# A token-projection stage whose weight units are loaded and split in halves, with its gates' row in three parts

## The reference

```python
def hybrid_layer(x, ...):
    h = rmsnorm(x, norm_pre_mix)
    proj = _f32(h @ w_in)
    u, z, xbc, dt_raw, qk, v, i_raw, f_raw, o_raw = jnp.split(proj, [int(o) for o in offs], axis=-1)
    y_a = s5_mixer(u, ...)                 # diagonal state space, then g * sigmoid(g @ w_glu + b_glu)
    y_b = ssd_mixer(z, xbc, dt_raw, ...)   # dt = softplus(dt_raw + dt_bias); acs = cumsum(dt * a, axis=2)
    y_c = mlstm_mixer(qk, v, i_raw, f_raw, o_raw, ...)   # log_sigmoid(f_raw + b_f), cumsum, running max
    mix = jnp.concatenate([y_a, y_b, y_c], axis=-1).astype(x.dtype) @ w_out
    x = x + rmsnorm(mix, norm_post_mix)
    h = rmsnorm(x, norm_pre_ffn)
    ff = (jax.nn.silu(h @ w_gate) * (h @ w_up)) @ w_down
    return x + rmsnorm(ff, norm_post_ffn)
```

## Time and profile before

| | us |
|---|---|
| median of 3 runs | 3132.67 |
| lowest, highest | 3131.85, 3136.79 |
| the profiled execution: its time | 3131.07 |
| the profiled execution: its span | 3129.3 |
| token stage, first to last matmul of its products | 577.3 to 1151.0 |
| PE busy, whole span | 2893.2 (92%) |
| DVE, ACT, POOL busy | 1905.5, 1198.4, 389.7 |
| mean granted TensorE clock | 0.964 of full speed |

### The profile page before, as it was taken

One profiled execution on the slowest core, in us unless ns is written; L12 is line 12 of the kernel. 1 busy time (PEld: TensorE's weight loads), 2 busy tenths in 40 slices (PEclk: granted clock), 3 DMA queues, 4 the chain that ended last, 5 costly groups with the idle time before them and its releaser, 6 DMA issues. The chain is left out here.

```text
span 3129.3 us, 35939 instructions
## 1 busy us (share of the span) xinstructions
PE 2893.2 (92%) x13608; PEld 2329.2 (74%) x13608; DVE 1905.5 (61%) x2572; ACT 1198.4 (38%) x1965; POOL 389.7 (12%) x495
## 2 busy tenths in 40 slices
PE   7999999689999775999789949999999999999998
PEld 4888887567776554777668848888878888888887
DVE  4777877565652216788434357666676666565756
ACT  5322222444342424455333344333443333454543
POOL 0000000013440006566202110000000000000100
PEclk9999999889999887999989979999999999999999
DMA  4222432336654537877477764444453222676863
GB/s 146 65 68 86 135 127 101 109 122 201 210 192 145 146 102 255 268 264 271 168 273 279 286 217 170 155 161 163 167 183 128 101 101 105 236 268 194 295 191 113
DMA packets 290105, 545.14 MB, mean 174 GB/s; under 512 B 58732, under 2 KB 150284, under 8 KB 276492
## 3 DMA queue, kind: packets, MB, share of 16 engines
q1 hardware_dynamic: 258172, 437.69, 41.4%
q0 software_dynamic: 24704, 75.52, 6.7%
q10 hardware_dynamic: 7056, 29.63, 2.4%
HBM read 358.30 MB, written 184.44 MB: 173 GB/s over the span
## 5 line engine op out<-in xcount | busy, mean ns | idle before, releaser
L2390 PE MATMUL f_banks<-f_bop,f_w_op 128*128 128x512 f32 x3696 | 842.9, 390 | 31.8 <-DVE f_w_op L2217 29.6
L2390 PEld LDWEIGHTS f_banks<-f_bop,f_w_op 128*128 128x128 f32 x3696 | 696.5, 189 | 178.2 <-DVE f_w_op L2217 30.0
L2398 PE MATMUL f_banks<-f_d_op 128*128 128x512 f32 x1848 | 419.0, 389 | 0.0
L2398 PEld LDWEIGHTS f_banks<-f_d_op 128*128 128x128 f32 x1848 | 346.8, 188 | 72.0
L1130 PE MATMUL t_banks<-t_w_hi,h_hi 128*128 128x512 f32 (+1 forms) x640 | 249.5, 390 | 31.7 <-DVE t_w_lo L1005 31.7
L2281 DVE TENSOR_TENSOR f_d_op<-f_d_raw,f_d_op 128x1024 fp32r<-128x1024 f32 x154 | 187.3, 1225 | 149.1 <-ACT f_d_op L2134 148.6
L640 PE MATMUL c_banks<-h_hi,c_w_hi 128*128 128x512 f32 x640 | 255.8, 400 | 0.0
L640 PE MATMUL c_banks<-h_hi,c_w_lo 128*128 128x512 f32 x640 | 249.9, 390 | 0.0
L640 PE MATMUL c_banks<-h_lo,c_w_hi 128*128 128x512 f32 x640 | 249.1, 389 | 0.0
L1130 PE MATMUL t_banks<-t_w_hi,h_lo 128*128 128x512 f32 (+1 forms) x640 | 239.6, 374 | 0.0
L1130 PE MATMUL t_banks<-t_w_lo,h_hi 128*128 128x512 f32 (+1 forms) x640 | 239.3, 374 | 0.0
(11 more groups left out here) (350 smaller groups left out, 4599.1 us busy)
## 6 DMA issues: line engine op xcount, KB each, us to landing
f_raw<-in_w_gu SPq DMA_DIRECT2D x88, 512.0 KB, 6.4
sop<-f_a SPq DMA_DIRECT2D x154, 256.0 KB, 2.0
f_d_raw<-sop SPq DMA_DIRECT2D x154, 256.0 KB, 2.8
t_raw<-in_w_tok SPq DMA_DIRECT2D x36, 1024.0 KB, 5.5
f_d_raw<-top SPq DMA_DIRECT2D x88, 256.0 KB, 4.2
m_bc<-rows SPq DMA_DIRECT2D x16, 1152.0 KB, 6.8
f_d_raw<-in_w_dn SPq DMA_DIRECT2D x66, 256.0 KB, 3.1
o_y_hi<-y_hi SPq DMA_DIRECT2D x16, 1024.0 KB, 5.1
```

Of the source, the lines that this page charges most:

```text
L2390: last = nc.tensor.matmul(bank[:, g, :], w_op[:, t % W_RING, w, cols], bop[:, s, h, k, :], start=begins and k == 0 and j == 0, stop=k == 3 ...
L2398: last = nc.tensor.matmul(banks[:, bank, :], d_op[:, d % D_RING, s, tok], d_op[:, d % D_RING, w, :], start=k == 0 and j == 0, stop=k == FU ...
```

## The change

Three things are changed in `phase_tokens`.

1. *Halves.* Load, `upper` and `lower` of a unit work on two halves of 1024 columns, first half in slot t=0, second half in slot t=1 of the unit ahead. There is a semaphore for the landing of each half (`raw_in[half]`), and `whi_ok` and `wlo_ok` count halves. A half of `t_raw` is loaded again as soon as `lower` has read that half. PE waits for the first half before the unit's first matmul, and in its first slot again before the first matmul that uses the second half.
2. *The row in three parts.* DVE's operations of slot 9c+0 are dealt out to slots 9c+0 (L1023 to L1037), 9c+1 (L1038 to L1046) and 9c+3 (L1048 to L1057), with the halves of `lower` in between where the slots fall on t=0 or t=1.
3. *Exponentials.* ACT's Ln and four Exp stand in slot 9c+5 instead of 9c+6, and both places with Exp and Ln load one table set that has both functions. That load stands behind the wait for `abs_ok` or `args_ok`.

The diff, without the changes of declaration:

```diff
@@ -805,10 +806,11 @@
 
         @block.sync
         def _(sp):
-            def load(unit):
+            def load(unit, half):
+                cols = slice(half * 2 * NB, (half + 1) * 2 * NB)
                 if unit:
-                    sp.wait_ge(wlo_ok, unit)
-                sp.dma_start(raw[:], w_tok[unit % UNITS_T]).then_inc(raw_in, 16)
+                    sp.wait_ge(wlo_ok, 2 * (unit - 1) + half + 1)
+                sp.dma_start(raw[:, cols], w_tok[unit % UNITS_T, :, cols]).then_inc(raw_in[half], 16)
 
             def gates(slot):
                 c, r = divmod(slot, GATE_STEP)
@@ -856,14 +858,16 @@
                 for dst, part in ((yhi_dram, y_hi), (ylo_dram, y_lo)):
                     sp.dma_start(dst[QT * b:QT * (b + 1), :, m, :].rearrange("n p t -> p n t"), chunks(part)).then_inc(part_sent, 16)
 
-            load(0)
+            load(0, 0)
+            load(0, 1)
             for dst, src in ((bias[:], gate_bias), (sign[:], gate_sign), (alog[:], gate_log), (ident_sb[:], ident), (bg[:], b_glu)):
                 sp.dma_start(dst, src).then_inc(const_in, 16)
-            load(1)
+            load(1, 0)
+            load(1, 1)
             for unit in range(UNITS):
-                if unit + 2 < UNITS:
-                    load(unit + 2)
                 for t in range(4):
+                    if t < 2 and unit + 2 < UNITS:
+                        load(unit + 2, t)
                     slot = 4 * unit + t
                     gates(slot)
                     if slot == GATE_STEP * BLK:
@@ -918,11 +922,12 @@
         def _(act):
             chain = Chain(act, act_chain)
 
-            def upper(unit):
-                act.wait_ge(raw_in, 16 * (unit + 1))
+            def upper(unit, half):
+                cols = slice(half * 2 * NB, (half + 1) * 2 * NB)
+                act.wait_ge(raw_in[half], 16 * (unit + 1))
                 if unit >= 2:
                     finished(act, unit - 2)
-                nc.scalar.activation(w_hi[:, unit % 2], raw[:], ACT.Copy).then_inc(whi_ok, 1)
+                nc.scalar.activation(w_hi[:, unit % 2, cols], raw[:, cols], ACT.Copy).then_inc(whi_ok, 1)
 
             def evac(e):
                 act.wait_ge(tile_mm, e + 1)
@@ -941,11 +946,13 @@
                         act.wait_ge(const_in, 80)
                         nc.scalar.activation(neg_a[:], alog[:], ACT.Exp).then_inc(neg_a_ok, 1)
                     act.wait_ge(abs_ok, c + 1)
+                    nc.scalar.preload_act_table_set("natural_log_exp_and_others")
                     nc.scalar.activation(e_, lnu, ACT.Exp, scale=-1.0).then_inc(exp_ok, 1)
                     act.wait_ge(one_plus_ok, c + 1)
                     nc.scalar.activation(lnu, u, ACT.Ln).then_inc(ln_ok, 1)
-                elif r == 6:
+                elif r == 5:
                     act.wait_ge(args_ok, c + 1)
+                    nc.scalar.preload_act_table_set("natural_log_exp_and_others")
                     chain(nc.scalar.activation(x[s_, :], x[s_, :], ACT.Ln))
                     chain(nc.scalar.activation(col_b[f, :], x[f, :], ACT.Exp))
                     chain(nc.scalar.activation(col_c, col_c, ACT.Exp))
@@ -976,12 +983,13 @@
                     act.wait_ge(part_sent, 32 * n)
                 nc.scalar.activation(y_hi.bitcast(F32R), y, ACT.Copy).then_inc(yhi_ok, 1)
 
-            upper(0)
+            upper(0, 0)
+            upper(0, 1)
             for unit in range(UNITS):
-                if unit + 1 < UNITS:
-                    upper(unit + 1)
                 n = group(unit)
                 for t in range(4):
+                    if t < 2 and unit + 1 < UNITS:
+                        upper(unit + 1, t)
                     slot = 4 * unit + t
                     if n is not None:
                         evac(QT * n + t)
@@ -1000,9 +1008,10 @@
                                  nc.vector.tensor_tensor_scan)
             mul, add, sub = ALU.mult, ALU.add, ALU.subtract
 
-            def lower(unit):
-                dve.wait_ge(whi_ok, unit + 1)
-                tt(w_lo[:, unit % 2], raw[:], w_hi[:, unit % 2].bitcast(F32), sub).then_inc(wlo_ok, 1)
+            def lower(unit, half):
+                cols = slice(half * 2 * NB, (half + 1) * 2 * NB)
+                dve.wait_ge(whi_ok, 2 * unit + half + 1)
+                tt(w_lo[:, unit % 2, cols], raw[:, cols], w_hi[:, unit % 2, cols].bitcast(F32), sub).then_inc(wlo_ok, 1)
 
             def gates(slot):
                 c, r = divmod(slot, GATE_STEP)
@@ -1035,6 +1044,7 @@
                     chain(scan(cum, mask, x, 0.0, mul, add))
                     end = chunks(cum)[:, :, P - 1]
                     chain(nc.vector.tensor_copy(ends[:, nxt], end))
+                elif r == 1:
                     chain(ts(u[f, :], gate_rows[IR:IR + HM, cols], bias[IR:IR + HM, :], None, add))
                     chain(tt(sp_[f, :], u[f, :], cum[f, :], sub))
 
@@ -1044,7 +1054,8 @@
                     m_end = chunks(run_max[f, :])[:, :, P - 1]
                     chain(nc.vector.tensor_copy(m_ends[f, nxt], m_end))
                     chain(tt(m_prev[f, tiles], m_ends[f, tiles], ends[f, tiles], add))
-
+                elif r == 3:
+                    end, m_end = chunks(cum)[:, :, P - 1], chunks(run_max[f, :])[:, :, P - 1]
                     chain(tt(chunks(x[f, :]), wide(m_prev[f, tiles], HM), chunks(run_max[f, :]), sub))
                     chain(ts(col_b, cum, -1.0, None, mul))
                     chain(ts(lnu[f, :], run_max[f, :], -1.0, None, mul))
@@ -1098,11 +1109,12 @@
                     dve.wait_ge(part_sent, 32 * n)
                 tt(y_lo.bitcast(F32R), y, y_hi, sub).then_inc(ylo_ok, 1)
 
-            lower(0)
+            lower(0, 0)
+            lower(0, 1)
             for unit in range(UNITS):
-                if unit + 1 < UNITS:
-                    lower(unit + 1)
                 for t in range(4):
+                    if t < 2 and unit + 1 < UNITS:
+                        lower(unit + 1, t)
                     slot = 4 * unit + t
                     gates(slot)
                     q = s5_step(slot)
@@ -1117,14 +1129,14 @@
             def products(unit, t):
                 b, i = divmod(unit, UNITS_T)
                 e = (b * GROUPS_T + i // 2) * QT + t
-                if t == 0:
-                    pe.wait_ge(wlo_ok, unit + 1)
                 begins, ends_ = i % 2 == 0, i % 2 == 1 or i == UNITS_T - 1
                 if begins and e >= QT:
                     pe.wait_ge(evac_ok, e - QT + 1)
                 k_first, ks, width = (i % 2 * 4, 4, NB) if i < UNITS_T - 1 else (0, KD, NB // 2)
                 tok = slice((b * QT + t) * P, (b * QT + t + 1) * P)
                 for k in range(ks):
+                    if t == 0 and k % (ks // 2) == 0:
+                        pe.wait_ge(wlo_ok, 2 * unit + k // (ks // 2) + 1)
                     cols = slice(k * width, (k + 1) * width)
                     for j, (h, w) in enumerate(((h_hi, w_hi), (h_lo, w_hi), (h_hi, w_lo))):
                         last = nc.tensor.matmul(banks[:, t, 0:width], h[:, k_first + k, tok], w[:, unit % 2, cols],
```

More of the change, by code:

```diff
@@ L756, in phase_tokens @@
         glu_bank = side[:, 0:2]
-        raw_in, whi_ok, wlo_ok, unit_mm, tile_mm, evac_ok = (
-            sem("t_" + s) for s in ("raw_in", "whi_ok", "wlo_ok", "unit_mm", "tile_mm", "evac_ok"))
+        whi_ok, wlo_ok, unit_mm, tile_mm, evac_ok = (
+            sem("t_" + s) for s in ("whi_ok", "wlo_ok", "unit_mm", "tile_mm", "evac_ok"))
+        raw_in = sem("t_raw_in0"), sem("t_raw_in1")
         out_sent = (sem("t_out_sent0"), sem("t_out_sent1"))
```

## The result

| | before | after |
|---|---|---|
| median, us | 3134.73 (4 runs, 3131.85 to 3140.19) | 3111.03 (4 runs, 3107.99 to 3113.06) |
| ratio, 95% interval | | 0.9922 [0.9904, 0.9939] |
| profiled execution: time, span | 3131.07, 3129.3 | 3112.76, 3111.0 |
| mean granted TensorE clock | 0.964 | 0.966 |

The account below looks back on a forecast made before the run. Up to 722 us a circle through DVE and ACT was taken as the bound, then PE. Gains of 14 to 16 us by chunk 3's transposes and 2 in the GLU, taken as 16.5 off 3132.67, gave 3116 us, range 3108 to 3126.

Parts of the forecast that it names:

- A circle through DVE and ACT: Up to 722 us: transposes, DVE's row, ACT's exponentials and DVE's products set the pace; gain 14 to 16 us by chunk 3.
- The new wait in unit 1: Chunk 0: PE waits about 2 us for the second half of `lower`, standing behind the row's first part.
- inside a chunk that is hidden by the circle: Stage up to S5: slow matmuls after the new stalls of 2 to 3 us cost nothing within a chunk.
- at most 1.6 us either way: Behind the last transposes: the most that a changed clock after stalls could cost or gain; counted as 0.
- The slack that the prediction names: DVE's row: half of `lower` often falls into a wait for ACT, 0.5 us a chunk, making the gain 13.8 to 16.
- The wait ahead of chunk 1's transposes: Chunk 1: PE idle some 5 us, more than the 3.90 before, since evacuation and unit 5's `upper` queue behind ACT's wait.
- The exponentials' earlier slot brings nothing: Chunk 1: no gain from the earlier slot, since ACT gets there before DVE.
- GLU: GLU groups: `load_g` leaves earlier at the second group, its 10.9 us wait shrinks by 2; 0 at first and third.
- The first, every chunk like chunk 1: Gates' chunks: evacuation and split stand in the circle each time, 33.6 us a chunk; gain 9.5, 3123 us; chance 0.18.
- The second, only the start: Stage up to S5: circle keeps its 34 us, gain 3.2 to at most 5, 3128 us; chance 0.08.
- The third, dearer table loads: Gates' stretch on ACT: five fewer loads each free another 1.3 us, 6.5 more gain, 3110 us; chance 0.06.
- The fourth, a collision with the S5 loads: S5 stretch: halves' loads delay the `u` tiles past 8.3 us, eating the gain, up to 3151 us; chance 0.06.

Follow-up runs that it names:

- e1_halves: The changed kernel with the row in one piece and the exponentials as before, so the halves alone; median 3129.19 us, ratio 0.9984 to the kernel before.
- e2_whole: The kernel before with the row in three parts and the exponentials' change, but units loaded and split whole; median 3133.26 us, ratio 0.9997 to the kernel before.
- e3_one_row: The changed kernel with the row in one piece in slot 9c+0; median 3123.09 us, ratio 0.9968 to the kernel before.
- e4_slot6: The changed kernel with the exponentials back in slot 9c+6 and table loads as before; median 3111.71 us, ratio 0.9933 to the kernel before.
- e10_slot6_hoist: The changed kernel with exponentials back in slot 9c+6 and both set loads ahead of their waits; median 3103.02 us, ratio 0.9902 to the kernel before.
- e9_sp_order: The kernel before with slot 116's load on SP moved behind send_y and load_g; median 3125.86 us, ratio 0.9973 to the kernel before.
- e6_step12: The changed kernel with GLU groups 12 slots apart instead of 10; median 3090.78 us, ratio 0.9858 to the kernel before.

## Why the prediction was right

**The mechanism held.** A circle through DVE and ACT paced the stage up to S5, and a shorter circle was given to PE. The marks, less the 0.9 us: start 574.4 (predicted 574.1), chunk 0 605.6 (605.3), chunk 1 638.2 (638.9), chunk 2 668.7 (670.0), chunk 3 697.4 (699.8). The new wait in unit 1 is 1.79 us (2). From S5's first matmul to the GLU's first it takes 209.3 us, as before, with PE busy throughout. A half of a unit took 1.05 us on ACT and 1.23 on DVE; all 72 halves landed after 3.4, 4.3 and 7.0 us (least, median, most). That the forecast needs both the halves and the parts of the row is what e1_halves, e2_whole and e3_one_row show.

**The clock, the term that was put at nothing.** The sum counted 14 to 16 us up to chunk 3's transposes, 13.8 by its marks, and nothing behind them; S5 begins 17.75 us earlier (730.20 against 713.35, and the 0.9). The step that failed is "inside a chunk that is hidden by the circle", said of the slower matmuls behind a stall. The transposes are a part of the circle: the 16 of chunks 1 and 2 took 1.94 us each time in the kernel before, behind waits of 3.90 and 4.76, and take 1.19 now, behind 2.90 and 3.03. So DVE begins the next row 1.2 and 1.3 us after their start, where 2.0 was taken over from before: 1.5 us in two chunks. The stretch behind the fourth transposes gives the other 1.6, for which the prediction allowed "at most 1.6 us either way" and counted 0; at chunk 3 there was no stall above 0.56 us.

**Smaller terms.** The set's load behind `abs_ok` lengthens the row by 0.5 us, not by the 0.9 that was charged: DVE's wait for the Exp grew from 0.77 to 2.05 us, but that for the Ln, 0.80, is gone, where 0.4 was taken off for it. The four rows together are 1.4 us shorter than was worked out. Behind chunk 0's transposes an evacuation was counted (0.6) that was already done. Against this stand 1.1 us: the first half came later than the 3.6 us counted (`upper` starts 3.95 after the issue), and in chunk 2 ACT reached its exponentials 0.84 us after `args_ok` (660.21 and 659.37), held by an evacuation that waited for a store of `t_out`. The slack that the prediction names, a half of `lower` that falls into a time in which DVE waits for ACT, is not in the rows: every half that it counted lay on the path.

**The wait ahead of chunk 1's transposes** was to be "about 5 us" and "more than the 3.90 of before"; it is 2.90. This step failed. ACT was indeed held at `args_ok` (3.94 us) with an evacuation and the `upper` of unit 5 behind it, but the second half of unit 4's `lower` stands behind the row's third part, and so 1.85 us of PE's idle time came as a wait of its own inside unit 4, which the prediction doesn't have. The two are 4.75 in sum.

**"The exponentials' earlier slot brings nothing"** was said of chunk 1 alone; e4_slot6 and e10_slot6_hoist show it of the whole stage as changed (with the row in one piece it brings 6 us). That a load of the set behind the wait costs time is shown: taking it out gives 5.5 us from the stage's first load to S5's first matmul (707.20 and 713.35, less 0.65 for the loads at 568.37 and 569.02) and 8.2 in the medians, for four chunks and two loads each.

**GLU.** 2 us at the second group and 0 at the others were predicted. The three waits were 5.79, 10.93 and 9.21 and are 5.29, 7.88 and 7.96, 4.8 less in sum, of which 3.4 reach the last product, because 1.4 us more of PE's time there was busy, at a clock of 0.93 instead of 0.94. It is the halves that do it, and at the second group: that wait was 10.93 in both profiled kernels with whole units and SP's old order, and is 7.2 to 8.3 in all six with halves, SP's order as changed and GLU groups 10 slots apart. Counted from the GLU's first matmul `load_g` leaves 1.6 us earlier (89.8 and 91.4 us), nearly the predicted 2; PE goes on 3.0 earlier, so 1.4 more lie between the issue and the landing, and no run tells why. The cause named, SP held by an unrelated load, is what e9_sp_order shows, and there was more in it than the 2 us of a half: all but 3.11 us of 10.93.

**The rivals.** The first, every chunk like chunk 1 at 33.6 us, is refuted by 30.56 and 28.71. The second, only the start, by the same. The third, dearer table loads, had the time nearest to the measured one (3110), so the time alone doesn't decide against it; the rows do. Ln starts 0.02 us after the load has ended (628.89 + 1.28 and 630.19), and ACT had been idle for 3.94 us ahead of that load; the next load, at 633.06, has its evacuation 0.01 us behind it. The stage has three table loads fewer, 50 instead of 53, not the five that the prediction counted; and e4_slot6, which has 53 again, takes the same time. The Trainium skill ("ScalarE: Activation LUTs", section "What ACT_TABLE_LOAD costs") adds about 1.4 us of drain to each; the rows here have none. The fourth, a collision with the S5 loads, didn't happen: the `u` tiles land after 5.6 us in the median and 7.0 at most (5.9 and 8.7 in the earlier trace rows), and PE waited 0.4 us for them, as before.

**The sum, and the luck in it.** Predicted 16.5, of which 14 to 16 up to chunk 3's transposes and 2 in the GLU. By rows it is 17.75 and 3.4, or 21.2, above the 16 to 18 of the sum; 3132.67 less that is 3111.5. The stages around took 2.9 us longer, which brings the profiled execution to 18.3 and near the forecast by chance. The medians differ by 23.7, 5 us more than the profiled executions, which lies within the ranges of both (4 runs each). And the range reaches down to 3108 only by adding the third rival's gain, which the rows refute: that it holds 3111 is in part luck, for the clock took up that room.

What stays open: what makes the stages around, whose code is the same, differ by up to 5 us from one profiled execution to the next, and what SP's order is worth in the time of a launch.

## What to carry to other kernels

Cut a transfer or a split in halves only together with the long serial work that stands between the halves in the same queue: here either one alone gave 5 and 1 us, and both 24. Where an engine's chain closes a circle with others, take out of it what needs none of its inputs, as the table set's load ahead of the semaphore wait (7 to 8 us here for moving two lines). Before shortening a wait, look in the issuing queue for a stranger ahead of the transfer that is waited for, and whether the schedule can simply give it more time: two more slots between the GLU groups were worth 20 us, beside the 24 of all of this change. And where a stall is followed by slower matmuls, ask whether these are a link of the circle, as the transposes are here: then a shorter stall pays twice.

## What was not expected of the hardware

A stall of PE mostly cost more than itself, by no fixed factor. 11.04 us of idle time fewer ahead of S5 came with 3.89 us less busy time for the same matmuls, and the granted clock rose from 0.91 to 0.94; in the GLU part 14.3 fewer came with 2.9 less (e6_step12, 0.93 to 0.97), but from the kernel before to the changed one 4.8 fewer with 1.4 more (0.94 to 0.93). What decides which stall is followed by a stretch at 1.2 GHz these runs don't tell apart.
